# Two recurrent mixers woven with dense products: which step of the weave their elementwise work stands in

## What is computed

```python
# HGRN2, from columns q, f of the input projection (lower bound 0)
q = silu(q_raw); k = 1 - sigmoid(f_raw); log_f = log(sigmoid(f_raw))
b = cumsum(log_f)                       # within chunks of 64 tokens
o = q*exp(b) @ state + sum_j (q_i . k_j . exp(b_i - b_j)) v_j

# RWKV-7, from eight 128-column tiles c: r (0,1), k (2,3), v (4,5), wd|ad (6), gd (7)
cm = c + (c_prev - c) * mu              # c_prev: one token earlier
w = exp(-exp(-softplus(-(w0 + tanh(wd) @ w2)) - 0.5)); a = sigmoid(a0 + ad @ a2)
g = sigmoid(gd) @ g2
kk = k*k_k; kk = kk / max(norm(kk), 1e-12); k = k*(1 + (a-1)*k_a)
state = state*w + (state @ -kk)(kk*a)^T + v k^T;  y = state @ r
```

## Time and profile before

| | us |
|---|---|
| median of 3 runs (1540.57 to 1545.72) | 1541.99 |
| profiled execution | 1547.78 |
| its span, first to last instruction | 1545.7 |
| TensorE busy (matmul) | 1499.2, 97% |
| VectorE busy | 1186.1, 77% |
| ScalarE busy | 869.7, 56% |
| granted TensorE clock, mean | 0.986 |

### The profile page before, as it was taken

One profiled execution on the slowest core, in us unless ns is written; L12 is line 12 of the kernel. 1 busy time (PEld: TensorE's weight loads), 2 busy tenths in 40 slices (PEclk: granted clock), 3 DMA queues, 4 the chain that ended last, 5 costly groups with the idle time before them and its releaser, 6 DMA issues.

```text
span 1545.7 us, 32239 instructions
## 1 busy us (share of the span) xinstructions
PE 1499.2 (97%) x10608; PEld 1332.3 (86%) x10608; DVE 1186.1 (77%) x2465; ACT 869.7 (56%) x1634; POOL 219.6 (14%) x167
## 2 busy tenths in 40 slices
PE   8799999999999899999999999999999999999997
PEld 8778887999877785798999999988888888888886
DVE  4788667889757577565499888889999777777777
ACT  5675545666558544665565566654444555555555
POOL 0001000011200001000078866620000000000000
PEclk9999999999999889999999999999999999999999
DMA  7434344565666610355567744467777666666665
GB/s 286 123 109 134 116 159 133 177 185 182 192 190 186 216 59 1 111 176 164 177 183 213 235 156 154 153 202 243 239 242 238 203 190 191 189 190 190 191 193 166
DMA packets 89292, 271.95 MB, mean 176 GB/s; under 512 B 9985, under 2 KB 27521, under 8 KB 88833
## 3 DMA queue, kind: packets, MB, share of 16 engines
q1 hardware_dynamic: 65520, 238.06, 49.3%
q10 hardware_dynamic: 23696, 32.87, 6.7%
HBM read 258.83 MB, written 12.06 MB: 175 GB/s over the span
## 4 chain that ended last, share of the span: by engine, by line
PE 89%; DVE 5%; ACT 3%; issue 1%; DMA 1%; ACTq 0%; DVEq 0%; SPq 0%
PE ps_chunk L508 17%; PE ps_misc L3049 12%; PE ps_chunk L501 10%; PE ps_misc L501 10%; PE ps_chunk L514 8%; PE ps_chunk L3166 7%; PE ps_misc L300 6%; PE ps_chunk L2000 4%; PE ps_chunk L3174 4%; PE ps_misc L2984 3%; PE ps_chunk L300 2%; PE ps_chunk L520 1%; DMA raw<-in_stream 1%; PE ps_misc L1027 1%; PE ps_chunk L529 1%
## 5 line engine op out<-in xcount | busy, mean ns | idle before, releaser
L425 ACT ACTIVATE w_hi<-raw 128x512 fp32r<-128x512 f32 (+2 forms) x654 | 399.9, 625 | 358.0 <-PE ps_chunk L514 143.4
L432 DVE TENSOR_TENSOR w_lo<-raw,w_hi 128x512 fp32r<-128x512 f32 (+2 forms) x516 | 352.5, 718 | 132.6 <-ACT w_hi L425 129.0
L508 PE MATMUL ps_chunk<-x_both,w_hi 128*128 128x256 f32 x2208 | 315.9, 285 | 0.5 <-ACT row L2875 0.5
L508 PEld LDWEIGHTS ps_chunk<-x_both,w_hi 128*128 128x128 f32 x2208 | 285.7, 192 | 0.9 <-issue 0.7
L432 POOL TENSOR_TENSOR w_lo<-raw,w_hi 128x512 fp32r<-128x512 f32 x140 | 182.2, 1314 | 257.6 <-DVE mixers_arena L2755 184.4
L514 PE MATMUL ps_chunk<-x_both,w_lo 128*128 128x256 f32 x1104 | 177.8, 283 | 0.0
L514 PEld LDWEIGHTS ps_chunk<-x_both,w_lo 128*128 128x128 f32 x1104 | 152.9, 193 | 0.0
L3264 DVE TENSOR_TENSOR w_lo<-raw,w_hi 128x512 fp32r<-128x512 f32 x120 | 83.0, 693 | 67.4 <-ACT w_hi L3218 67.3
L501 PE MATMUL ps_chunk<-w_hi,x_both 128*128 128x512 f32 (+1 forms) x392 | 124.0, 398 | 7.5 <-DVE w_lo L432 7.5
L3166 PE MATMUL ps_chunk<-x_both,w_hi 128*128 128x512 f32 x480 | 120.2, 392 | 0.0
L3218 ACT ACTIVATE w_hi<-raw 128x512 fp32r<-128x512 f32 x120 | 75.7, 631 | 63.5 <-PE ps_misc L501 63.3
(11 more groups left out here) (442 smaller groups left out, 2586.5 us busy)
## 6 DMA issues: line engine op xcount, KB each, us to landing
raw<-in_stream SPq DMA_DIRECT2D x452, 512.0 KB, 3.8
early_rows<-row ACTq DMA_DIRECT2D x68, 128.0 KB, 2.8
row<-early_rows ACTq DMA_DIRECT2D x66, 128.0 KB, 3.3
memory_kv<-mixers_arena ACTq DMA_DIRECT2D x4, 512.0 KB, 4.6
mixers_arena<-in_cmp_w ACTq DMA_DIRECT2D x1, 2048.0 KB, 11.0
mixers_arena<-memory_kv ACTq DMA_DIRECT2D x4, 512.0 KB, 6.3
row<-in_rows ACTq DMA_DIRECT2D x3, 512.0 KB, 5.4
mixers_arena<-in_consts ACTq DMA_DIRECT2D x1, 1441.0 KB, 8.1
```

The lines of the kernel that those rows point to most:

```text
L425: e.activation(w_hi[q % 2][:, s], raw[q][:, s], ACT.Copy).then_inc(made, 1)
L432: e.tensor_tensor(w_lo[q % 2][:, s], raw[q][:, s], w_hi[q % 2][:, s].bitcast(F32), ALU.subtract).then_inc(made, 1)
L508: e.matmul(o, w[0][:, k * P:(k + 1) * P], x[:, k, :], start=k == 0 and x is x_hi, stop=False, skip_group_check=True)
```

## The change

It touches the weave's string and two generators. In RWKV: a Tanh on one column is put in front of the step (its table is then loaded there); tiles 6 and 7 are shifted and mixed first, tiles 0 to 5 are shifted in the next step, and are mixed two at a time in the three steps after it; the block from the decay on is a step of its own; B - LW is made there, into PX; the four Exps stand by the head_ones product, in front of the Sqrt; the reciprocal is two of 256 columns, each with a step of its own. In HGRN: the five ScalarE operations get four steps in place of one, the memset of S goes to POOL, the first products wait for ScalarE alone, and the masked copies for the memsets too. The string has 422 letters in place of 415: three h and four r more, as many d (242).

```diff
@@ hgrn
             yield from evacuated(4, act, dve)
+            pool.do(lambda e: e.memset(S, 0.0))
             cleared = pool.do(lambda e: e.memset(KL, 0.0))
             act.do(lambda e: e.activation(LF, zf, ACT.Abs))
             act.do(lambda e: e.activation(LF, LF, ACT.Exp, scale=-1.0))
+            yield
             a = act.do(lambda e: e.activation(LF, LF, ACT.Ln, bias=c("one")))
+            yield
             act.do(lambda e: e.activation(K, zf, ACT.Sigmoid, scale=-1.0))
-            act.do(lambda e: e.activation(zq, zq, ACT.Silu))
+            yield
+            with_k = act.do(lambda e: e.activation(zq, zq, ACT.Silu))
...
-            dve.do(lambda e: e.memset(S, 0.0))
-
 
             for level in range(-1, LEVELS):
                 if level < 0:
-                    q_l, k_l, mask, v = zq, K, by_block[:, LEVELS, :], dve.now()
+                    q_l, k_l, mask, v = zq, K, by_block[:, LEVELS, :], None
...
-                        done = pe.do(mm(ps[chunk, i * HG_C:(i + 1) * HG_C], k_l[:, of_both], q_l[:, of_both]), v, act.now(),
-                                     *free)
+                        done = pe.do(mm(ps[chunk, i * HG_C:(i + 1) * HG_C], k_l[:, of_both], q_l[:, of_both]),
+                                     *([v, act.now()] if v else [with_k]), *free)
...
-                    ps.rearrange("p (a b) -> p a b", b=HG_C)), done)
+                    ps.rearrange("p (a b) -> p a b", b=HG_C)), done, cleared)
@@ rwkv
-            dve.do(lambda e: e.tensor_tensor(shift[:, :, 1:T], zc[:, :, 0:T - 1], zc[:, :, 1:T], ALU.subtract))
-            dve.do(lambda e: e.tensor_scalar(shift[:, :, 0:1], zc[:, :, 0:1], -1.0, None, ALU.mult))
-            for k in (6, 7, 0, 1, 2, 3, 4, 5):
-                if k == 0:
-                    low_rank = dve.now()
...
+            act.quiet(lambda e: e.activation(ss[:, 15:16], c("one"), ACT.Tanh))
+
+            def shifted(some):
+                dve.do(lambda e: e.tensor_tensor(shift[:, some, 1:T], zc[:, some, 0:T - 1], zc[:, some, 1:T], ALU.subtract))
+                dve.do(lambda e: e.tensor_scalar(shift[:, some, 0:1], zc[:, some, 0:1], -1.0, None, ALU.mult))
+
+            def mixed_in(*tiles):
+                for k in tiles:
...
+            shifted(slice(6, 8))
+            mixed_in(6, 7)
+            low_rank = dve.now()
...
             a = act.do(lambda e: e.activation(sg, CM[:, 7, :], ACT.Sigmoid))
+            shifted(slice(0, 6))
...
+                mixed_in(2 - 2 * j, 3 - 2 * j)
                 yield
...
+            mixed_in(4, 5)
             banks.release(gate_at, 1, g_tok)
 
+            yield
             dve.do(lambda e: e.tensor_scalar(LW, LW, -RK_DECAY_SCALE, None, ALU.mult), a)
...
+            centred = dve.do(lambda e: e.tensor_tensor(PX, B, LW, ALU.subtract))
...
             done = pe.do(mm(ps, head_ones, X2), v, *free)
+            act.do(lambda e: e.activation(PX, PX, ACT.Exp), centred)
+            act.do(lambda e: e.activation(X3, B, ACT.Exp))
+            yield
+            act.do(lambda e: e.activation(EL[:, 0:2], EL[:, 0:2], ACT.Exp))
+            powers = act.do(lambda e: e.activation(X1, B, ACT.Exp, scale=-1.0), gdone)
             yield
             a = act.do(lambda e, ps=ps: e.activation(X2, ps, ACT.Sqrt), done)
             banks.release(at, 1, a)
             dve.do(lambda e: e.tensor_scalar(X2, X2, 1e-12, None, ALU.max), a)
-            dve.do(lambda e: e.reciprocal(X2, X2))
+            for s in (slice(0, T), slice(T, 2 * T)):
+                dve.do(lambda e, s=s: e.reciprocal(X2[:, s], X2[:, s]))
+                yield
...
             yield
-            v = dve.do(lambda e: e.tensor_tensor(X2, B, LW, ALU.subtract))
-            act.do(lambda e: e.activation(X2, X2, ACT.Exp), v)
-            act.do(lambda e: e.activation(X3, B, ACT.Exp))
-            act.do(lambda e: e.activation(EL[:, 0:2], EL[:, 0:2], ACT.Exp))
-            yield
-            a = act.do(lambda e: e.activation(X1, B, ACT.Exp, scale=-1.0), gdone)
-            dve.do(lambda e: e.tensor_tensor(PX, KK, X2, ALU.mult), a)
+            dve.do(lambda e: e.tensor_tensor(PX, KK, PX, ALU.mult), powers)
```

More of the change, by code:

```diff
@@ L63 @@
 SUMS = ((0, 1, 16, 0), (1, 1, 8, 16), (2, 2, 8, 24), (4, 4, 4, 40), (8, 8, 1, 56))
[L65 to L69, removed]
+MIXERS_ORDER = ("ddddddddddddddddddddddddddmmddddddddddddrrrddddddrdrdrmrddrddddmrdrddrddrddrdddrddrdddddhhddhddhddrd"
+                "dhddrhdrdhrrddhddhdrdhmdhdddddrhdhhdrhrrhddrddddhdrhhrdddhhdddrdhddhdddhrrdhdddhrhdddhhddhdhddrddrhd"
+                "dhhdrdddrhhdrrrmmmhhrrmmrrrddddhdrdhrrhddrhhrddhhhhddhhhddhdrhddhhhrrhhhhrhhhrdhhdhdddddhhhhddhdddhh"
+                "ddddrdrddddhddrhrdrdrdhdhrddddhrhrddddhddddrdrdddhrrrrhddrddhdrhrhhrhrdhddddddrddddhddddddddrddddddd"
+                "drrdddddrddddddddddrhm")
 MEMORY_ORDER = ("dddnddddndddndndddddddaaddabbdddaabddabdddbaddbdaddaabeebbbedffeddddfddeddfddddddfedddfeeffddeeffddddddd"
@@ L1535, in rwkv @@
                 lane.wait(loaded[12])
-            dve.do(lambda e: e.tensor_tensor(shift[:, :, 1:T], zc[:, :, 0:T - 1], zc[:, :, 1:T], ALU.subtract))
-            dve.do(lambda e: e.tensor_scalar(shift[:, :, 0:1], zc[:, :, 0:1], -1.0, None, ALU.mult))
-            for k in (6, 7, 0, 1, 2, 3, 4, 5):
-                if k == 0:
-                    low_rank = dve.now()
-                dve.do(lambda e, k=k: e.scalar_tensor_tensor(out=CM[:, k, :], in0=shift[:, k, :], scalar=c("rwkv_mu", k),
-                                                             in1=zc[:, k, :], op0=ALU.mult, op1=ALU.add))
+            act.quiet(lambda e: e.activation(ss[:, 15:16], c("one"), ACT.Tanh))
[4 more added lines that the diff above has]
+                for k in tiles:
+                    dve.do(lambda e, k=k: e.scalar_tensor_tensor(out=CM[:, k, :], in0=shift[:, k, :],
+                                                                 scalar=c("rwkv_mu", k), in1=zc[:, k, :], op0=ALU.mult,
+                                                                 op1=ALU.add))
+            shifted(slice(6, 8))
+            mixed_in(6, 7)
+            low_rank = dve.now()
             rr, kk, vv = (CM[:, 2 * n:2 * n + 2, :] for n in range(3))
```

## The result

The changed kernel took 1576.12 us, the median of four runs (1574.34 to 1581.63), beside 1541.28 for the kernel before: ratio 1.0234, 95% interval 1.0207 to 1.0261, or +36 us (34.8 us by the two medians) where +2.8 was forecast. Its profiled execution took 1575.01 us (span 1573.0).

A forecast was written before the change was run, and what follows sets the result against it. TensorE, busy 97% of the span, was taken to bound the kernel, and VectorE the stretch changed. Waits, lost cover and clock summed to 14.8 us against 12.0, +2.8 us: 1541.99 becomes 1544.8 us, range 1537 to 1549.

The forecast's parts named there:

- Low-rank tiles first: RWKV's gate: the 2.65 us wait goes, and the low half of unit 11's split comes 0.4 us late.
- Mixes over dense steps: Behind unit 12: TensorE waits 3.2 us for the square, in place of 2.31 us before that unit.
- Reciprocal in halves: RWKV's transposes behind unit 15: TensorE waits 6.2 us for the last product, until 74.0 us.
- HGRN's five operations: HGRN on ScalarE: waits of 1.5 us for split 19 and 0.85 us for Silu, replacing 1.94 + 0.34.
- the 0.85 us for Silu: HGRN's h7 products: TensorE reaches them at 91.6 us, Silu ends at 92.4, a wait of 0.85 us.
- The bound: From 42.4 us VectorE's work lasts to 71.6, so TensorE idles at least 7.5 us; spreading doesn't shorten it.
- The clock: Falls to half clock behind the new waits: between 0 and 3.3 us, taken as one fall of 1.65 us.
- slower: Rival, 28%: 6 us wait at the transposes, two clock falls, cover lost in full; +5.6 us, 1547.6 us.
- How to follow the steps: Method of the walk: 2.9 us a unit, queue by queue; four inserted letters bring the rest one step forward.
- The order string: Six d steps moved ahead find nothing to do before memory's transposes: between 0 and 2.2 us, taken as 1.0.
- the sum: All terms in the mixers stage: 14.8 us after the change against 12.0 before, +2.8 us.
- The gain that I thought possible in the tail: Behind RWKV's norm: one r step more of lead may spare 1.99 + about 1.7 us; within a 15% rival.

The follow-up runs named there:

- y1: The changed code in an order string without the six d steps ahead or later r and h steps brought forward: 1539.09 us beside 1540.18, ratio 1.0007.
- y2: The kernel before with only the low-rank tiles shifted and mixed first, the others spread over the next RWKV steps, old string: ratio 1.0009.
- y4: y1 with the four exponentials behind the Sqrt, beside the two halves of the reciprocal, one r letter fewer: ratio 1.0002.
- x3: The kernel before with one r letter more amid unit 18 (a unit is four d steps) and the last r taken off: 1574.98 us, ratio 1.0222.
- z4: y1 with the additional r step alone, from unit 18 on, no dense steps ahead: 1570.83 us, ratio 1.0193.
- w3: z2 with one pair of letters exchanged (rh becomes hr) at unit 47, moving one VectorE instruction behind the windows' softmax: ratio 1.0114.
- x2: The kernel before with six d letters moved from the string's end to amid unit 18, nothing else: 1549.17 us, ratio 1.0054.
- z2: The kernel before with RWKV one step ahead only from unit 32 to the end of the stage: 1570.49 us, ratio 1.0153.
- x4: The changed code with a string that puts every piece of work where the old string had it, no lead: 1549.65 us, ratio 1.0063.
- z1: The kernel before with RWKV one step ahead from unit 18, given back at unit 32: 1547.16 us, ratio 1.0039.
- w1: The kernel before with RWKV one step ahead from unit 32 to unit 41 only, given back at unit 42: ratio 1.0065.
- w2: The kernel before with RWKV one step ahead from unit 42 to the end: ratio 1.0095.

## Why the prediction was wrong

**The part walked was nearly right.** "Low-rank tiles first": 0.37 us for w_lo at 45.92, forecast 0.4. "Mixes over dense steps": 2.73 us for the square, forecast 3.2. "Reciprocal in halves": 5.39 us at the transposes at 72.0, forecast 6.2 at 74. "HGRN's five operations": 1.66 us before unit 19, forecast 1.5; the 0.85 us for Silu didn't come. TensorE idles 10.2 us from 42 to 104, where 0.4 + 3.2 + 6.2 + 1.5 + 0.85 = 12.15 was forecast and 10.1 was before: the idle time of this stretch didn't change. The bound (VectorE has as much to do, and spreading doesn't shorten it) is in line with y1, y2 and y4, where the wait comes back elsewhere, and the time of all four stays within 0.3%.

**"The clock", mis-sized.** I took one fall of 1.65 us. By the clock column of the table above, 0.12 × 14 + 0.34 × 10 + 0.22 × 14 + 0.02 × 12 = 8.4 us were lost to it between 42 and 104 us, against 0.17 × 10 = 1.7 before. Around and behind the 5.39 us wait the clock was 0.55 for 7 us:

```profile
68.00:75.00 7.00, 2.98 (x14) 2.98 (x15) 4.80 (x8) 1.32 (x3) 0.00 (x0) 0.55 0.21 77
```

I had let a fall cost the same behind any wait. And that the 2.65 us wait had no fall behind it, on which I built, was chance: x3 has the same instructions in the same order up to 84 us, waits 2.65 us there too, and runs at half clock right behind. First the kernel before, then x3:

```profile
49.50:52.50 3.00, 3.00 (x21) 2.52 (x22) 1.29 (x2) 2.90 (x7) 0.00 (x0) 1.00 0.01 3
```
```profile
47.00:50.00 3.00, 2.88 (x10) 1.98 (x11) 1.29 (x2) 2.25 (x6) 0.00 (x0) 0.50 0.01 3
```

The rival "slower" had the mechanism with two falls (3.3 us) and was still short. From 42 to 104 us the clock took 8.4 − 1.7 = 6.7 us more than before, of the 36.

**The step that failed: the r step of lead, put at nothing.** "How to follow the steps" says that the inserted letters "bring the rest one step of content forward". "The order string", where the cost of that belonged, prices only the six d steps, and the sum has no term for it. That rest is 170 us of woven work, in which the three strands share in-order queues. The first memory transposes came at 152.27 us, where 141 to 144 was forecast. x3 alone prices it at 34 us, z4 again at 31, and w3 with the rows of the changed kernel shows one instance: the step's evacuation blocks VectorE for another strand. The same step priced the six d steps ahead at 1.0 of at most 2.2 us; x2 has 4.5 us by the stage end and 8 timed. TensorE idles 3.9 us from 104 to 140 in x2, against 0.23: I had counted the cover that is missing where the six d steps find nothing to do, not what the other strands' waits become behind it; which of them makes x2's 8 us was not taken apart.

**The sum** of the parts measured apart: y1's 0, the r step's 34, the d steps' 8 make 42 us where the change has 36. They overlap: the r step costs 34 in the kernel before but 23.5 on top of everything else in the change.

**The rival with the right sign** put slower on the transposes at 68 us. The wait is there, but y1 has it too (4.97 us) and isn't slower. So even its 28% were for a wrong reason. The gain that I thought possible in the tail from one r step more of lead is refuted: from unit 32 on the lead costs 22.8 us (z2).

**Left open.** In x3 the cost is spread over at least eight waits; one of them was taken apart (w3, made on z2 and not on the changed kernel, whose rows show the same pair of waits), the others only by stretch (z1, w1, w2). Most times lie further above the kernel before than the stage ends do (x2 8 us against 4.5, y1 +1 against −4.1). A good part of that is the one profile of the kernel before, which is 2.4 us late at the first split: counted from that split, x2's stage is 5.8 us longer, y1's 1.8 shorter, x3's 32.7, z2's 23.9 and x4's 5.2 longer. What remains is open. The 7 us by which the code behind the stage varies are mostly clock as well: half clock takes 9.5 to 11.5 us of it in the five profiles where that code is shortest, and 14.8 to 14.9 in the five where it is longest. Why the clock falls more often in one execution than in another wasn't found.

**Which version is best.** None of these beats the kernel before by more than the measurement can tell; y1 (1539.1 beside 1540.2 us) equals it.

## What to carry to other kernels

In a schedule woven by an order string, an inserted letter is not local: it moves every later step of its strand against the others, and that shift needs a walk of its own to the end of the stage, or the string must be brought back to its old alignment right behind the edit. When you move a step on an in-order engine, look at its first instruction that waits and ask what of other strands is queued behind it; placing it earlier helps nobody if its input comes no earlier. Price a gap together with the clock behind it: here each of the 21 waits of TensorE over 3 us that the 17 profiles have between 42 us and the stage end had 3 to 9 us of half clock behind it.

## What the runs showed of the hardware

What I had not expected was the size of the clock's part. In the kernel before half clock takes 3.4 us of the stage; in the changed kernel it takes 20.5, and this rise of 17.1 us stands beside 22.5 us of added idle time. Where TensorE idled, half clock cost nothing: counted only where it was at work, the rise is from 3.4 to 17.4 us. 14.0 + 22.5 = 36.5 us is the whole of what the stage grew by, counted from the first split (36.6). In z2, x3 and z4 half clock takes 15.4, 17.1 and 18.8 us of the stage, in w1 10.2, w2 13.7, y1 5.1. The length of a wait alone doesn't tell whether a fall follows: in the changed kernel the clock stayed whole behind the 2.71 us wait at 151.66, and was at half from 161 to 164 us behind the 1.98 us wait at 160.07. Nor do the instructions decide it alone, as x3 beside the kernel before has shown: nine kernels have the same lists up to 84 us, and the 2.65 us wait near 48 us had half clock within 2 us behind it in seven of their profiles and none in two (the kernel before and z2).

A table load cost ScalarE 1.28 us with the ACTIVATE right behind it, in the changed kernel too, and y4, with two loads fewer than y1, was no faster. The Trainium skill, page "ScalarE: Activation LUTs", section "What ACT_TABLE_LOAD costs", has 2.66 us for a switch with its drain; no run here shows the drain, and the measured 1.28 us decides. Here are the last Exp, the load and RWKV's Sqrt, in the changed kernel:

```profile
56.43 0.63 ACT L1609 ACTIVATE mixers_arena<-mixers_arena 128x512 f32<-128x512 f32 x1
57.13 1.28 ACT L1611 ACT_TABLE_LOAD   x1
58.43 0.60 ACT L1611 ACTIVATE mixers_arena<-ps_misc 128x512 f32<-128x512 f32 x1
```

The Exp ends at 57.06 and the load starts at 57.13; the load ends at 58.41 and the Sqrt starts at 58.43: no drain lies between them.
